# Moving two modulation vectors' weight tiles from the first expert layer to the second mixer

## What is computed

```
mods = jnp.einsum('bd,lde->lbe', jax.nn.silu(c), ada_w) + ada_b[:, None, :]
for layer in range(DEPTH):
    sh1, sc1, g1, sh2, sc2, g2 = jnp.split(mods[layer], 6, axis=-1)
    h = modulate(rms_norm(x, norm_g[layer, 0]), sh1, sc1)
    ...                                    # layer 0: conv_fox_mixer, layer 1: nsa_mixer
    x = x + g1[:, None, :] * y
    h = modulate(rms_norm(x, norm_g[layer, 1]), sh2, sc2)
    x = x + g2[:, None, :] * peer_ffn(h, peer_w_q[layer], ...)
```

## Time and profile before

| | us |
|---|---|
| median of 3 runs | 3912.07 (3908.88 to 3912.6) |
| the profiled execution, device time | 3912.14 |
| its span, first to last instruction | 3910.3 |
| PE busy in the span | 3481.9 (89%) |
| DVE busy | 2581.1 (66%) |
| ACT busy | 1695.0 (43%) |
| POOL busy | 596.3 (15%) |
| peer0's last part | about 844 to 1225 |
| mix1 | about 1230 to 1510 |

### The profile page before, as it was taken

One profiled execution on the slowest core, in us unless ns is written; L12 is line 12 of the kernel. 1 busy time (PEld: TensorE's weight loads), 2 busy tenths in 40 slices (PEclk: granted clock), 3 DMA queues, 4 the chain that ended last, 5 costly groups with the idle time before them and its releaser, 6 DMA issues.

```text
span 3910.3 us, 59393 instructions
## 1 busy us (share of the span) xinstructions
PE 3481.9 (89%) x23498; PEld 3095.7 (79%) x23498; DVE 2581.1 (66%) x4435; ACT 1695.0 (43%) x2711; POOL 596.3 (15%) x389
## 2 busy tenths in 40 slices
PE   5579789999998788978999999897988999878899
PEld 5459778888887657967888999896867989777698
DVE  5647868877775744986886655557665545567554
ACT  2234324444443434432444444444644444445443
POOL 0038620000000035942000000000121000010300
PEclk9789879999999979988999999999998999999899
DMA  6425313457776402522445655553333555533255
GB/s 215 135 96 164 124 63 121 148 176 242 248 235 202 143 22 82 178 82 66 149 148 192 214 185 187 156 188 122 107 105 118 185 160 183 158 112 113 87 168 172
DMA packets 161122, 581.88 MB, mean 149 GB/s; under 512 B 19024, under 2 KB 21072, under 8 KB 160720
## 3 DMA queue, kind: packets, MB, share of 16 engines
q1 hardware_dynamic: 156528, 569.66, 45.5%
q10 hardware_dynamic: 3744, 7.85, 0.6%
q0 software_dynamic: 576, 0.57, 0.1%
HBM read 576.44 MB, written 1.05 MB: 148 GB/s over the span
## 4 chain that ended last, share of the span: by engine, by line
PE 68%; DVE 21%; ACT 6%; issue 3%; DMA 2%; POOL 1%; ACTq 0%; DVEq 0%
PE P L1717 17%; PE P L685 17%; PE P L1692 12%; PE P L710 11%; PE P L1679 4%; DVE LOW L492 2%; ACT HI L479 1%; DMA RING<-in_pu 1%; DVE ssd_a L2366 1%; DVE peer_oh L1949 1%; DVE peer_eq L1947 1%; DVE peer_a L1853 1%; DVE peer_a L1855 1%; DVE peer_a L1859 1%; DVE peer_a L1857 1%
## 5 line engine op out<-in xcount | busy, mean ns | idle before, releaser
L492 DVE TENSOR_TENSOR LOW<-RING,HI 128x1024 fp32r<-128x1024 f32 x844 | 1021.9, 1226 | 352.0 <-ACT HI L479 351.0
L479 ACT ACTIVATE HI<-RING 128x1024 fp32r<-128x1024 f32 x988 | 1031.8, 1053 | 297.8 <-DMA RING<-in_fdB 59.7
L492 POOL TENSOR_TENSOR LOW<-RING,HI 128x1024 fp32r<-128x1024 f32 x144 | 376.9, 2629 | 300.1 <-ACT HI L479 299.9
L685 PE MATMUL P<-HTH,LOW 128*128 128x256 f32 x2400 | 352.0, 290 | 69.7 <-DVE LOW L492 69.6
L685 PE MATMUL P<-HTH,HI 128*128 128x256 f32 x2400 | 365.0, 296 | 32.3 <-ACT HI L479 16.2
L685 PEld LDWEIGHTS P<-HTH,LOW 128*128 128x128 f32 x2400 | 317.5, 197 | 82.4 <-DVE LOW L492 82.2
L685 PEld LDWEIGHTS P<-HTH,HI 128*128 128x128 f32 x2400 | 326.2, 199 | 45.9 <-issue 21.2
L685 PE MATMUL P<-HTL,HI 128*128 128x256 f32 x2400 | 349.7, 290 | 0.0
L685 PEld LDWEIGHTS P<-HTL,HI 128*128 128x128 f32 x2400 | 323.2, 200 | 0.0
L1692 PE MATMUL P<-HTH,HI 128*128 128x256 f32 x2048 | 309.3, 292 | 7.2 <-ACT HI L479 7.1
L1692 PE MATMUL P<-HTH,LOW 128*128 128x256 f32 x2048 | 310.1, 297 | 4.8 <-POOL LOW L492 4.8
(11 more groups left out here) (403 smaller groups left out, 5366.6 us busy)
## 6 DMA issues: line engine op xcount, KB each, us to landing
RING<-in_pu SPq DMA_DIRECT2D x256, 512.0 KB, 3.6
RING<-in_pv SPq DMA_DIRECT2D x256, 512.0 KB, 3.6
RING<-in_ada SPq DMA_DIRECT2D x96, 512.0 KB, 4.0
RING<-in_fgA SPq DMA_DIRECT2D x44, 512.0 KB, 3.6
RING<-in_fuA SPq DMA_DIRECT2D x44, 512.0 KB, 3.5
RING<-in_fdA SPq DMA_DIRECT2D x44, 512.0 KB, 3.6
RING<-in_fgB SPq DMA_DIRECT2D x44, 512.0 KB, 3.5
RING<-in_fuB SPq DMA_DIRECT2D x44, 512.0 KB, 3.5
```

The costliest lines, as they stand in the source:

```text
L479: act.activation(c.his[i % NHL], c.raw[m % NR], ACT.Copy).then_inc(*c.hi.at(("hi", m)))
L492: eng.tensor_tensor(c.low[m % NR], c.raw[m % NR], c.his[i % NHL].bitcast(F32), ALU.subtract).then_inc(*sig.at(("lo", m)))
L685: m = pe.matmul(ps[:, 0:256], w[:, k * 128:k * 128 + 128], c.ht[h][:, k, :], start=i == 0 and k == 0, stop=i == 2 and k == 7)
```

## The change

The order of the pieces changes, and with it the place of two of them. Before, peer0 runs the pieces 6, 7, 9, 10, 5 (behind pv0 64 to 113) and mix1 runs piece 8. After, peer0 runs 6, 7, 5 (behind pv0 64 to 93) and mix1 runs 8, 9, 10: piece 9 starts behind nsaq 2, its slots 0 to 4 stand behind nsaq 3 to 7, and from there on two steps stand behind each of the tiles nsao 0 to 5: (9 slots 5, 6), (9 slot 7, 9 last), (10 first, 10 slot 0), (10 slots 1, 2), (10 slots 3, 4), (10 slots 5, 6). What is left, slot 7 and "last" of 10, stands at the end of the stage.

```diff
-SUMS = (2, 3, 4, 6, 7, 9, 10, 5, 8, 11)
+SUMS = (2, 3, 4, 6, 7, 5, 8, 9, 10, 11)
...
-    todo = of(6, 7, 9, 10, 5)
+    todo = of(6, 7, 5)
     spread(todo, [(("pv0", j), 1) for j in range(64, 127)])
     after["end", "peer0"] = todo
-    todo = of(8)
-    spread(todo, [(("nsac", j), 1) for j in range(8)] + [(("nsaq", j), 1) for j in range(8)])
+    todo = of(8, 9, 10)
+    spread(todo, [(("nsac", j), 1) for j in range(8)] + [(("nsaq", j), 1) for j in range(8)]
+           + [(("nsao", k), 2) for k in list(NSA_SLOTS[0].values())])
     after["end", "mix1"] = todo
```

## The result

The changed kernel took 3941.72 us (median of 4 runs, 3938.67 to 3949.4) beside 3910.69 us for the kernel before on the same chip (4 runs, 3908.88 to 3912.6). The ratio over all runs is 1.0084 (it is not the quotient of the two medians, which are 31.0 us apart), with a 95% interval of 1.0069 to 1.0099, so +33 us, between +27 and +39. Run once more on another occasion, unchanged, it gave 1.0086 (1.0072 to 1.0099), with medians 36 us apart. The forecast was 3938.0 in a range of 3922 to 3954, and slower with a chance of 0.87.

What follows compares the result with a forecast made beforehand. PE was taken to bound peer0's last part, DVE mix1's query projections, and a PE-DVE-ACT-DVE loop the attention. Terms -8.2 + 18.2 + 15.7 = +25.7 us took the median from 3912.07 to 3938, range 3922 to 3954.

Steps and rivals of the forecast that it cites:

- peer0, -8.2: Peer0's last part: taking out two pieces' slots, loads, firsts and lasts gains 8.2 us, between 3.7 and 10.
- Projections, +18.2: Mix1's query projections: added DVE slots and low parts made late, so L788 waits for PE; 18.2 us, between 14.3 and 20.7.
- three slow passes of five: Projections: three of five third passes run at slow clock, adding 3 x 1.29 to 14.3 us.
- Attention and end, +15.7: Mix1's attention output slots and stage end: waits for parts and the bias load add 15.7 us, bounds 12 and 22.
- slot 1, high part and "last": Attention, behind nsao 0: PE waits 1.96 us for ACT's high part, then runs piece 9's "last", 1.84; together 3.8 us.
- slot 2, bias load: Attention: DVE's first slot of piece 10 waits for POOL's memset and bias load, delaying the next item; 3.9 us.
- slot 4, high part, slot 5, high part: Attention: PE waits for ACT's late high part, 1.96 us; the two DVE slots just fit below it.
- end: End of mix1: slot 6's high part is late and piece 10's "last" stands before the residual on DVE; 3.3 us.
- The moved work hides: Rival: moved slots and late parts cost no wait, only peer0's gain stays; 3904 us, chance 0.05.
- Half of it hides: Rival: projections cost only DVE slots (6.4 us), attention only slots 1 and 2 (7.7); 3916 to 3918 us, chance 0.07.
- The clock falls for long: Rival: PE's waits keep it at 1.2 GHz for most of the attention, costing 14.5 us; 3952 us, chance 0.13.

Runs made afterwards that it cites:

- busy_pe: The changed kernel with 12 extra unused matmuls on PE ahead of each of the five waiting third passes of nsaq 4 to 7 and nsak 0; ratio 1.0067.
- after_again: The changed kernel run and profiled once more, unchanged, to see which waits and clock falls come again; ratio to the kernel before 1.0086.
- tiny_slots: The changed kernel with the 16 DVE slots of pieces 9 and 10 cut to 8 of 1024 columns, tiles and loads kept; 3933.84 us, ratio 1.0064.
- piece9_only: The kernel before with piece 9 alone moved from peer0 to mix1, at the same places as in the change; ratio 1.0055.
- piece10_only: The kernel before with piece 10 alone moved to mix1, two steps behind each of nsao 0 to 4; ratio 1.0045.
- the first repair: The changed kernel with ACT's and DVE's look-ahead in nsaq and nsao counted over split tiles only, skipping modulation tiles; 3928.26 us, ratio 1.0055.
- first_early: The changed kernel with the memset and bias load of piece 10 moved from output slot 2 to slot 1; 3931.6 us, ratio 1.0063.
- all_mended: The changed kernel with look-ahead mended, piece 10's bias load in slot 1, its slots behind nsao 2 to 5, its "last" behind the residual; 3915.77 us, ratio 1.0016.

## Why the prediction was right, step by step

**peer0, -8.2.** Eight executions have this code: -6.7, -6.9, -7.3, -8.1, -8.2, -10.1, -10.2, -12.6, in the mean -8.8. Right in size. The bound of -10 was too tight (three of the eight lie beyond it), and the half alone gave -5.0 (piece 9) and -9.2, -6.4 and -6.1 (piece 10), so it isn't 4.1 per piece to the microsecond; what spreads it I didn't find.

**Projections, +18.2.** 19.1, 19.7, 19.3 and 18.9: the mechanism, the place (L788, now L789, of the five tiles behind nsaq 3) and the size were right. My choice of three slow passes of five was a little low: four took 1.97 to 2.08 in after, the fifth 1.61: it began with the clock still at 1.00, which fell to 0.50 in the middle of the pass (1.00 from 1296.50 to 1297.00, 0.50 from 1297.50 on). The rule of the Trainium skill (TensorE: Matmul & The Clock Gate, "HAM oscillation — how this bites in real kernels") had all five slow, 20.7; the trace lies between it and my 18.2, and busy_pe agrees that the waits matter, since with less idling ahead of them the passes came nearer to full clock.

**Attention and end, +15.7.** Measured 26.0 and 24.5, beyond my own upper bound of 22: this is the term that was mis-sized. Read from the times of the 32 reciprocals (L997), forecast, then after, after_again:

| place | forecast | after | after_again |
|---|---|---|---|
| before item 0 (clock rises later) | 0 | 2.5 | 0.4 |
| slot 0 | 0 | 0 | 0 |
| slot 1, high part and "last" | 3.8 | 3.7 | 3.7 |
| slot 2, bias load | 3.9 | 4.7 | 5.3 |
| falls of the clock between slots | 0 | 3.4 | 5.1 |
| slot 3 | 0.8 | 0.9 | 0.9 |
| slot 4, high part | 1.96 | 3.6 | 2.05 |
| slot 5, high part | 1.96 | 2.05 | 3.6 |
| end | 3.3 | 4.9 | 3.5 |

The waits are where the prediction put them, and half of them are right to 0.2 us. What is missing (10.3 and 8.8 us) is mostly clock, 8.9 and 7.1 by this table; the rest is slot 2, whose wait I put 0.8 to 1.4 too low. The prediction named the clock as the upper bound ("above, if PE's clock falls in the wait of slot 2", 7 us) and then left it out of the sum. That wait is one place of the fall, as in after, but not the only one, as after_again showed. The price per us was too high: I had 7 us for 20 at the low rate, and here some 13 us cost 3.4 to 3.7. The clock is also inside slots 4 and 5: one of the two, a different one each time, takes 3.6, because PE's passes behind the wait for ACT run partly at half clock. From the timeline of after, slot 4:

```profile
1486.84 1.17 PE L711 MATMUL P<-HI,mix_h 128*128 128x512 f32 x4 [1.80 <-ACT HI L480]
1487.85 1.60 PE L711 MATMUL P<-HI,mix_l 128*128 128x512 f32 x4
1489.25 1.91 PE L711 MATMUL P<-LOW,mix_h 128*128 128x512 f32 x4
```

The wait of 1.80 is close to the 1.96 that I had worked out from ACT's row, and 1.60 and 1.91 stand for passes of 1.08. At the end 1.4 us more came the same way in after (the clock is at 0.50 from 1519 to 1522, in the last items' products); after_again has no low clock there, and its 3.5 is near the forecast. PE waited 1.51 us for slot 6's high part, as forecast, and the last of 10 and the residual ran as foretold: L569 from 1529.01, the residual from 1531.05.

**The sum.** 25.7 forecast, 37.8 and 37.5 by stages, 33 and 34 by the ratios. The direction, two of three terms and the places were right, the attention's 7 to 9 us of clock were not in it. That 3938 came within 4 us of 3941.72 is partly luck: by stages the forecast is 12 us short, by the ratios 7 to 8. The two profiled spans are only 30.2 us apart, because the execution of before was 11.8 us slower ahead of the first mark; after was 4.2 slower behind the last.

**The rivals.** "The moved work hides" is what tiny_slots, piece9_only and piece10_only rule out. "Half of it hides" fell with the third passes. "The clock falls for long" was nearest: it is not 40 us more of low clock, but some 13 us of it at a place that varies, and shorter spells behind some of the waits.

## What to carry to other kernels

Work that is put between steps costs more than its own time where something counts positions: here a distance in the stream, which the inserted tiles used up, was two thirds of the cost in the projections. So ask of each inserted item whose look-ahead, ring place and queue it takes, and mend it engine by engine: the first repair moved the wait to another engine, because the ring had no place for it. And a step that costs waits also costs clock: where the trace of before shows both levels of the clock in a stage, put a fall of it into the sum, not only into its bound.

## What the runs showed of the hardware that I had not expected

**GpSimd and VectorE hold each other up.** DVE's multiply-add with two operands in SBUF takes 1.28 us, but 3.44 beside a low part on POOL; POOL's scalings, 0.60 and 0.93 us, take 1.61 and 2.78 beside two DVE slots and the low part on DVE that follows them (1444.87 to 1446.09). From the timelines of after (end) and all_mended (slot 2, then the end):

```profile
1525.10 2.69 POOL L493 TENSOR_TENSOR LOW<-RING,HI 128x1024 fp32r<-128x1024 f32 x1 [7.71 <-ACT HI L480]
...
1525.43 3.44 DVE L537 SCALAR_TENSOR_TENSOR ACC<-RING,MOD,ACC 128x1024 f32<-128x1024 f32 x1
```

```profile
1442.28 2.67 DVE L537 SCALAR_TENSOR_TENSOR ACC<-RING,MOD,ACC 128x1024 f32<-128x1024 f32 x2
...
1442.43 1.61 POOL L1023 TENSOR_SCALAR mix_a<-mix_a,STAT 128x128 f32<-128x128 f32 x1 [1.04 <-DVE STAT L1005]
...
1444.02 2.78 POOL L1024 TENSOR_SCALAR mix_a<-mix_a,STAT 128x256 f32<-128x256 f32 x1
...
1508.79 4.81 POOL L493 TENSOR_TENSOR LOW<-RING,HI 128x1024 fp32r<-128x1024 f32 x2 [7.03 <-ACT HI L480]
...
1511.26 2.89 DVE L761 TENSOR_TENSOR X<-X,mix_a 128x512 f32<-128x512 f32 x1
```

The Trainium skill (SBUF — State Buffer, "SBUF: two separate sides") says that the two share a pair of ports which one holds for a whole instruction, and that a DVE instruction needs it, against a GpSimd instruction that reads SBUF, when it reads two operands from SBUF. The trace agrees: in the residual of all_mended, beside POOL's low parts, L758, with one operand in PSUM, kept its 0.69, while L761 behind it, with both in SBUF, took 2.89 instead of 0.69.

**The clock can fall while PE is fully busy**, by the rows of after_again above: 2.00 of 2.00 us busy, at 1.00, then 0.50 for some 13 us of fully busy PE. A late effect of the idling before (1.80 us, ended 6.5 us ahead of the fall) isn't excluded. Against it: after, first_early and piece9_only have the same wait of 1.80 at slot 1, and their clock stays at 1.00 for 24, 46 and 82 us behind it. No run here tells what sets it off.
